# One decoder layer in fp32 products on one core: mixer-norm modulation in quarters, 28 projection units between its loads, and one fp32 product behind each down projection

## The reference

```
mod = silu(c) @ w_mod + b_mod                 # c: 2048, w_mod: 2048 x 12288
sh_a, sc_a, g_a, sh_f, sc_f, g_f = split(mod, 6)
hmix = rms_norm(x, gain) * (1 + sc_a) + sh_a  # 512 x 2048
proj = hmix @ w_in                            # split into u, gla_q, gla_k, gla_v, gla_g, gla_low,
                                              # nsa_q, kc, vc, ksl, vsl, kwn, vwn, nsa_g
mix  = concat(pool_mixer(u), gated_linear_attention(...), nsa_attention(...)) @ w_out
x = x + g_a * mix
hf = rms_norm(x, gain_f) * (1 + sc_f) + sh_f
x = x + g_f * ((silu(hf @ w_gate) * (hf @ w_up)) @ w_down)      # hidden width 5632
```

## Time and profile before

| | us |
|---|---|
| median of 3 runs (2625.59 to 2627.77) | 2626.35 |
| the profiled execution | 2625.79 |
| its span, first to last instruction | 2623.9 |
| TensorE busy | 2488.2 |
| VectorE, ScalarE, GpSimd busy | 893.6, 779.3, 1148.0 |

### The profile page before, as it was taken

One profiled execution on the slowest core, in us unless ns is written; L12 is line 12 of the kernel. 1 busy time (PEld: TensorE's weight loads), 2 busy tenths in 40 slices (PEclk: granted clock), 3 DMA queues, 4 the chain that ended last, 5 costly groups with the idle time before them and its releaser, 6 DMA issues.

```text
span 2623.9 us, 33211 instructions
## 1 busy us (share of the span) xinstructions
PE 2488.2 (95%) x11481; PEld 2028.5 (77%) x11481; DVE 893.6 (34%) x1413; ACT 779.3 (30%) x1482; POOL 1148.0 (44%) x894
## 2 busy tenths in 40 slices
PE   5589999999789999979999999999999999999999
PEld 3577777887688888858888888888888888888887
DVE  4765332258576677771202020201020202010102
ACT  2023224232456622233222222222222222222221
POOL 0024323444576634434444444444444444444443
PEclk8579999999799999989999999999999999999999
DMA  8742223365211177742232323322332332332333
GB/s 298 258 147 81 64 68 103 113 237 180 85 49 57 65 250 256 259 159 95 97 97 96 95 89 96 96 89 94 96 90 94 96 94 90 96 96 89 95 96 112
DMA packets 86221, 315.96 MB, mean 120 GB/s; under 512 B 9584, under 2 KB 10240, under 8 KB 84736
## 3 DMA queue, kind: packets, MB, share of 16 engines
q1 hardware_dynamic: 84240, 303.31, 35.5%
q10 hardware_dynamic: 1904, 11.62, 1.2%
HBM read 310.69 MB, written 4.19 MB: 120 GB/s over the span
## 4 chain that ended last, share of the span: by engine, by line
PE 63%; issue 24%; POOL 10%; DVE 2%; ACT 0%; POOLq 0%; ACTq 0%; DVEq 0%
PE ps L429 57%; POOL wlo L342 9%; PE ps L769 2%; PE ps L758 1%; PE ps L726 1%; PE ps L727 1%; DVE macc L1203 1%; POOL qn L362 0%; DVE biasT L1490 0%; PE ps L712 0%; PE ps L750 0%; POOL kn L367 0%; POOLq L341 0%; PE ps L741 0%; POOL pmod L385 0%
## 5 line engine op out<-in xcount | busy, mean ns | idle before, releaser
L342 POOL TENSOR_TENSOR wlo<-raw,whi 128x512 fp32r<-128x512 f32 x728 | 964.0, 1326 | 1365.5 <-ACT whi L894 1103.2
L894 ACT ACTIVATE whi<-raw 128x512 fp32r<-128x512 f32 x612 | 385.9, 632 | 1260.6 <-PE ps L429 1127.7
L429 PE MATMUL ps<-hfH,whi 128*128 128x512 f32 x1408 | 559.0, 397 | 17.1 <-DVE hfL L1620 13.1
L429 PE MATMUL ps<-hfL,whi 128*128 128x512 f32 x1408 | 558.8, 397 | 0.0
L429 PE MATMUL ps<-hfH,wlo 128*128 128x512 f32 x1408 | 558.3, 397 | 0.0
L429 PEld LDWEIGHTS ps<-hfH,whi 128*128 128x128 f32 x1408 | 266.5, 189 | 80.8 <-issue 13.9
L429 PEld LDWEIGHTS ps<-hfH,wlo 128*128 128x128 f32 x1408 | 266.4, 189 | 61.4
L429 PEld LDWEIGHTS ps<-hfL,whi 128*128 128x128 f32 x1408 | 266.6, 189 | 60.9
L1647 DVE SCALAR_TENSOR_TENSOR x1T<-ps,modc,x1T 128x512 f32<-128x512 f32 x176 | 132.1, 751 | 455.9 <-PE ps L429 455.9
L429 PE MATMUL ps<-huH,whi 128*128 128x512 f32 x704 | 279.2, 397 | 0.5 <-DVE huL L1631 0.5
L429 PE MATMUL ps<-huL,whi 128*128 128x512 f32 x704 | 279.1, 396 | 0.0
(11 more groups left out here) (262 smaller groups left out, 2926.7 us busy)
## 6 DMA issues: line engine op xcount, KB each, us to landing
raw<-in_wstream SPq DMA_DIRECT2D x370, 512.0 KB, 3.6
modw<-in_mstream SPq DMA_DIRECT2D x192, 512.0 KB, 4.6
xT<-in_xt SPq DMA_DIRECT2D x4, 1024.0 KB, 8.2
w1s<-in_w ACTq DMA_DIRECT2D x2, 2048.0 KB, 8.3
x1T<-in_xt ACTq DMA_DIRECT2D x4, 1024.0 KB, 8.6
out_y<-x1T SPq DMA_DIRECT2D x16, 256.0 KB, 2.0
cmpb<-in_cmp_tab ACTq DMA_DIRECT2D x1, 1024.0 KB, 7.1
ptab<-in_tabs ACTq DMA_DIRECT2D x1, 768.0 KB, 5.1
```

The lines of the kernel that those rows point to most:

```text
L342: nc.gpsimd.tensor_tensor(wlo[:, s, :], raw[:, r, :], whi[:, s, :].bitcast(F32), ALU.subtract).then_inc(unit_ready, 1)
L429: ins = nc.tensor.matmul(acc, lhs, rhs, start=first and n == 0, stop=last and n == 2)
L894: A(whi[:, k % SPLIT, :], raw[:, k % 8, :], ACT.Copy).then_inc(unit_hi, 1)
```

## The change

- **Order of the modulation.** The quarters now come as shift 0, scale 0, shift 1, scale 1 and so on, so that after two quarters (16 tiles) four row blocks of x can be modulated.
- **Who computes.** Of each of the 64 tiles VectorE takes only one half of 512 columns (`pre_mod`). Of the other half TensorE takes 128 columns with one product. For the other 384 ScalarE multiplies in place (`scale_rows`) and GpSimd adds into `pacc2` (`add_scaled`). A quarter is closed by seven products in place of four. The accumulators are double.
- **The ring.** It has eight tiles (`modw` and `modx`); a place comes free when VectorE, TensorE and GpSimd are done with it. `scale_rows` stands on ScalarE behind the root L905.
- **Units between loads.** 28 units stand ahead of the blocks: per four row blocks 4 units of gla_q and gla_k, one narrow unit and 2 units of kc. Twenty of them stand between the tiles, from tile 20 on, seven to sixteen tiles (`STEP_UNIT`), their splits on ScalarE and GpSimd two tiles later (`STEP_SPLIT`). 13 unit loads stand between the tile loads on SyncE's queue (`UNIT_LOADS`). The other eight units follow. The fourth block shrinks to 8 units for vc alone, with two `beside` calls behind each.
- **`keep_busy`.** Behind each tile without a unit TensorE makes fp32 products of ones by ones, 128 x 64 by 128 columns, into an unused part of PSUM: six each for tiles 8 to 15, then three each.
- **FFN.** Behind the down projection of each of the ten rounds TensorE makes one fp32 product of identity and ones into bank 1, ahead of the up tile. It waits for `up_saved` at the value for which the up tile waits anyway.
- The five loads of tables on ScalarE's queue move from behind L905 to behind the last rounding of x.

```diff
+        STEP_UNIT = {16 * (u // 7 + 1) + (4, 6, 8, 11, 13, 15, 17)[u % 7]: u for u in range(20)}
+        STEP_SPLIT = {step + 2: u + 4 for step, u in STEP_UNIT.items() if step + 2 < 64}
+        STEP_SPLIT.update({10 + u: u for u in range(4)})
+        UNIT_LOADS = (8, 10, 14, 18, 22, 26, 35, 40, 44, 49, 53, 57, 60)
...
+            def load_pre(m):
+                if m >= 8:
+                    sp.wait_ge(mod_used, m - 7)
+                    sp.wait_ge(mod_pe, m - 7)
+                    sp.wait_ge(mod_pool, m - 7)
+                sp.dma_start(pre_tile(m), mstream[m * P:(m + 1) * P, :]).then_inc(pre_landed[m % 8], 16)
...
+            def add_scaled(m):
+                q, d = m // 8, m % 8
+                if d == 0 and q >= 2:
+                    pool.wait_ge(mod_summed, q - 1)
+                pool.wait_ge(mod_scaled, m + 1)
+                src = pre_tile(m)[:, P:U]
...
+                    ins = TT(pacc2[q % 2][:, :], pacc2[q % 2][:, :], src, ALU.add)
+                ins.then_inc(mod_pool, 1)
+            for m in range(64):
+                add_scaled(m)
+                if m in STEP_SPLIT:
+                    low_part(STEP_SPLIT[m])
...
+            def keep_busy(count):
+                for n in range(count):
+                    nc.tensor.matmul(ps[64:128, 4, 0:P], ones[:, 0:64], ones[:, :], start=True, stop=True,
+                                     skip_group_check=True)
...  in modulate(q), on TensorE:
+                    nc.tensor.matmul(acc[:, 0:1], pre_tile(m)[:, 0:P], cact[:, 2 * d:2 * d + 1], start=d == 0, stop=False,
+                                     skip_group_check=True).then_inc(mod_pe, 1)
                     if beside is not None:
                         beside(d)
+                    elif m in STEP_UNIT:
+                        first_unit(STEP_UNIT[m])
+                    else:
+                        keep_busy(6 if m < 16 else 3)
                 pe.wait_ge(mod_used, 8 * q + 8)
...  four products with pacc, then
+                pe.wait_ge(mod_pool, 8 * q + 8)
+                for j in range(3):
+                    ins = nc.tensor.matmul(acc[:, 1 + j:2 + j], pacc2[q % 2][:, j * P:(j + 1) * P], ones[:, 0:1],
+                                           start=False, stop=True, skip_group_check=True)
...
                 gate_tile(base, 4 * j + 4, 0)
                 down_tiles(base + 4, j)
+                pe.wait_ge(up_saved, 4 * j + 3)
+                nc.tensor.matmul(ps[:, 1, 0:P], ident[:, :], ones[:, :], start=True, stop=True)
                 up_tile(base + 20, 4 * j + 4, 0)
...  on ScalarE, behind the root L905:
+            def scale_rows(m):
+                act.wait_ge(pre_landed[m % 8], 16 * (m // 8 + 1))
+                part = pre_tile(m)[:, P:U]
+                A(part, part, ACT.Copy, scale=cact[:, 2 * (m % 8):2 * (m % 8) + 1]).then_inc(mod_scaled, 1)
+            for m in range(64):
+                scale_rows(m)
+                if m >= 16 and 2 <= m % 16 < 6:
+                    hm_high(4 * (m // 16 - 1) + m % 16 - 2)
+                if m in STEP_SPLIT:
+                    split(0, STEP_SPLIT[m], STEP_SPLIT[m] + 1)
...  on VectorE:
+            pre_mod(0)
             dve.wait_ge(sq_summed, KD)
             own(V.tensor_scalar(xvar[:, :], ps[:, 0, :], 1.0 / D, EPS, ALU.mult, ALU.add))
             V.reciprocal(xvar[:, :], xvar[:, :]).then_inc(var_ready, 1)
+            pre_mod(1, lambda: pre_columns(0))
+            normalise_rows(0)
+            for kq in range(1, 4):
+                def last_rows():
+                    pre_columns(2 * kq - 1)
+                    modulate_rows(kq - 1)
+                pre_mod(2 * kq, last_rows)
+                normalise_rows(kq)
+                pre_mod(2 * kq + 1, lambda: pre_columns(2 * kq))
+            pre_columns(7)
+            modulate_rows(3)
```

More of the change, by code:

```diff
@@ L30 @@
 FAR = 1e30
-UNITS_IN = 16 + 4 + 8 * KD
+UNITS_IN = 28 + 7 * KD + 8
 UNITS_OUT = 4 * KD
@@ L135, in layer_kernel @@
         modw = at("modw", [P, 4, 2 * U], F32, qk_base)
+        modx = at("modx", [P, 4, 2 * U], F32, xs_base)
         macc = at("macc", [P, U], F32, lg_base)
+        pacc = [at(f"pacc{i}", [P, U], F32, pbase + (40 + 2 * i) * KB) for i in range(2)]
+        pacc2 = [at(f"pacc2{i}", [P, 3 * P], F32, pbase + 44 * KB + i * 1536) for i in range(2)]
         place[0] = pbase + 24 * KB
@@ L449, in token_block, with value_block @@
                     after(k)
[L451 to L456, removed]
+            def value_block(u0, after):
+                for j in range(8):
+                    s = j % SPLIT
+                    pe.wait_ge(unit_ready, u0 + (j + 1))
+                    for kk in range(2):
+                        k = 2 * j + kk
+                        for c in range(2):
+                            if k == 0:
+                                pe.wait_ge(proj_saved, 12 + c + 1)
+                            col = slice((2 * kk + c) * P, (2 * kk + c + 1) * P)
+                            ins = passes(ps[:, c, :], hmH[:, k, :], hmL[:, k, :], whi[:, s, col], wlo[:, s, col],
+                                         False, k == 0, k == KD - 1)
+                            if k == KD - 1 and c == 0:
+                                ins.then_inc(tile_done, 1)
+                    ins.then_inc(unit_used, 1)
+                    after(2 * j)
+                    after(2 * j + 1)
@@ L474, in modulate @@
                 for d in range(8):
[L475 to L479, removed]
+                    m = 8 * q + d
+                    pe.wait_ge(pre_landed[m % 8], 16 * (m // 8 + 1))
@@ L500, in _ @@
             modulate(0, square_pair)
-            with pe.Fori(1, 8) as i:
-                modulate(i)
+            modulate(1)
+            for q in range(2, 8):
+                modulate(q)
+            for u in range(20, 28):
+                first_unit(u)
             def sum_columns(q, bank):
@@ L911, in _ @@
                 act.dma_start(dst, src).then_inc(gla_const, 16)
[L912 to L920 removed]
+            split(0, 23, 29)
             for c in range(4):
@@ new lines, in pre_mod, with pre_columns, modulate_rows @@
+                    dve.wait_ge(mod_used, m + 1)
+                    if d == 1 and inside is not None:
+                        inside()
+            def pre_columns(q):
+                dve.wait_ge(mod_summed, q + 1)
+                V.tensor_tensor(modc[:, 4 * q:4 * q + 4], ps[:, 7, 4 * (q % 2):4 * (q % 2) + 4],
+                                vec[:, V_B + 4 * q:V_B + 4 * q + 4], ALU.add).then_inc(mod_read, 1)
+                dve.wait_ge(mod_read, q + 2)
+            def modulate_rows(kq):
+                own(V.scalar_tensor_tensor(out=acol[:, 4 * kq:4 * kq + 4], in0=modc[:, 8 * kq + 4:8 * kq + 8], scalar=1.0,
+                                           in1=vec[:, V_GMIX + 4 * kq:V_GMIX + 4 * kq + 4], op0=ALU.add, op1=ALU.mult))
+                dve.wait_ge(xn_ready, 4 * kq + 4)
+                for k in range(4 * kq, 4 * kq + 6):
+                    if k < 4 * kq + 4:
+                        V.tensor_scalar(xT[:, k, :], xT[:, k, :], acol[:, k:k + 1], modc[:, 8 * kq + k % 4:8 * kq + k % 4 + 1],
+                                        ALU.mult, ALU.add).then_inc(hm_full, 1)
+                    if k >= 4 * kq + 2:
+                        dve.wait_ge(hm_hi, k - 1)
+                        V.tensor_tensor(hmL[:, k - 2, :], xT[:, k - 2, :], hmH[:, k - 2, :].bitcast(F32),
+                                        ALU.subtract).then_inc(hm_ready, 1)
@@ L1234, in _, with normalise_rows @@
+            def normalise_rows(kq):
+                dve.wait_ge(std_ready, 1)
+                for k in range(4 * kq, 4 * kq + 4):
+                    V.tensor_tensor(xT[:, k, :], xT[:, k, :], xrstd[:, :], ALU.mult).then_inc(xn_ready, 1)
             dve.wait_ge(cact_ready, 1)
-            with dve.Fori(0, 2) as i:
-                own.enter(i, 8)
-                half_mod(i)
-            own.leave(2)
+            pre_mod(0)
             dve.wait_ge(sq_summed, KD)
```

261 lines of the change are left out of this document (147 added, 114 removed).

## The result

| | before | after |
|---|---|---|
| median (4 runs each, same chip) | 2627.06 us | 2599.93 us |
| lowest to highest | 2625.59 to 2630.04 | 2594.21 to 2602.03 |
| profiled execution, its span, mean granted clock | 2625.8, 2623.9, 0.962 | 2594.2, 2592.4, 0.977 |

The ratio is 0.9892, 95% interval [0.9876, 0.9907]: 27.1 us faster. The forecast gain was 54.4 us, with a range of 2558 to 2597, which the median misses by 3 us.

A forecast was written before the change was run, and what follows sets the result against it. TensorE was taken as the bound, its large work held back until 156.56 us by the ring of four tiles. 2625.8 - 44 (modulation) - 13.4 (FFN pace) + 3.0 (products) = 2571.4, stated as 2572 us; range 2558 to 2597.

The forecast's parts named there:

- Until tile 8: Start of the kernel: tile 8 can't load before about 41.8 us; GpSimd's eight steps end at 49, quarter 0 at 50.4.
- Tiles 8 to 19: Modulation ahead of the units: quarter 1 closed at 66.9 us, about 4 us more, unit 0 starting at 71 us.
- Tiles 20 to 63: Tiles with units between: 87.3 us of TensorE at full clock plus 6 us of waits, ending at 164.3 us.
- lumps of 1.5 and 0.5 us: TensorE's waits in tiles 20 to 63: 1.5 us for each of three quarters, 0.5 for the other three, 6 us.
- Behind them: From the tiles' end at 164.3 us: unit 20 in effect at 168.3 against 212.93, a gain of about 44 us.
- the three terms of the forecast: Behind the tiles: unit 21 waiting for rows 1 us, five loads delaying unit 23's split 2 us, kc copies 1 us.
- The FFN: Ten FFN rounds: faster pace in eight stretches gains 13.4 us, the fp32 products cost 3.0 us.
- Rival 1: FFN: the product does not reset the pace and 3.0 us are paid for nothing; 2585 us, chance 0.21.
- Rival 2: Modulation: VectorE and GpSimd become the bound, about 22 us of the gain go; 2594 us, chance 0.12.
- a third of a lock: VectorE's multiply-adds beside GpSimd: 1.11 us against 0.75, read as a partial exclusion and not a whole one.
- Rival 3: TensorE's clock stays at half from tile 8 to the tiles' end, 102 us more; 2674 us, chance 0.04.
- Rival 4: TensorE waits less than counted, GpSimd at 0.75 us and no waits at quarter ends; 2560 us, chance 0.07.

The follow-up runs named there:

- experiment 5: Changed kernel with ScalarE scaling the first eight tiles between its squares instead of behind the root: 2592.33 us.
- Experiment 4: Changed kernel with VectorE reading the even quarter's columns before it normalises the rows: 2591.68 us.
- experiment 3: Changed kernel without the 120 idle products of ones by ones: 2585.78 us.
- experiment 7: Changed kernel without idle products, with columns read before the normalisation and the first eight tiles scaled between the squares: 2572.59 us.
- experiment 8: Changed kernel with columns read before the normalisation and the first eight tiles scaled between the squares, idle products kept: 2587.32 us.
- experiment 1: Kernel before with only the ten fp32 products of identity and ones behind the down projections added: 2615.92 us.
- experiment 2: Kernel before with only the wait for up_saved, 2631.7 us; and with ten fp32r products in place of fp32 ones, 2608.1 us; single runs.
- experiment 6: Changed kernel with GpSimd's 56 additions cut from 384 to 8 columns, leaving out the rest of its sums: 2589.84 us.
- the fp32r kernel: Kernel before with ten fp32r products of hfH behind the down projections: 2608.1 us in its single run.

## Why the prediction was half right

**Until tile 8: right.** Forecast: tile 8 at 41.8, GpSimd's sum at 49. Measured 40.78 and 48.70. That `scale_rows(0)` stands behind the root and blocks SyncE was shown by experiment 5. Also right was that the ring frees the loads: 388 GB/s.

**Tiles 8 to 19: 6.3 us short.** Unit 0 came at 77.27, not 71. Closing quarter 1 began at 67.23, where I had 65.5, and took 2.05 us and not 1.4. Steps 16 to 19 took 69.28 to 77.27 = 8.0 us instead of 4, since the clock was at its half level from 69.8 to 80.1 us. I had it at full from about 54 us to the end.

**Tiles 20 to 63: the step that failed.** Forecast 93.3 us (87.3 of work at full clock and 6 of waits), measured from unit 0 to unit 20 194.72 - 77.27 = 117.5. The missing 24.1 us, by distances from start to start:

| part | forecast | measured | more |
|---|---|---|---|
| clock at half for 23.3 of the 117.5 us | 0 | five units of 3.7 to 4.6 us in place of 2.83, and steps beside them | 8.2 |
| waits of TensorE | 6 | 8.3 for columns (5 times) + 4.8 for pacc (twice) = 13.1 | 7.1 |
| tile products and idle products, at full clock | 8.8 + 15.1 | 29.6 | 5.7 |
| units, at full clock | 55.0 | 20 of 2.83 = 56.6 | 1.6 |
| closing a quarter (six times), without its waits | 8.4 | 9.9 | 1.5 |

The waits were a term that I gave in lumps of 1.5 and 0.5 us and never traced. The first product of quarter q + 1 waits at L564 for the columns of the quarter before it to be read; VectorE reads them at step 1 of its own next quarter, and in the odd ones it has four rows to normalise ahead of that. VectorE's timeline in after:

```profile
125.50 3.97 DVE L1377 TENSOR_TENSOR xT<-xT,xrstd 128x512 f32<-128x512 f32 x4
129.40 0.47 DVE L1343 TENSOR_SCALAR pacc<-modw,cact 128x512 f32<-128x512 f32 x1
129.91 0.75 DVE L1345 SCALAR_TENSOR_TENSOR pacc<-modw,cact,pacc 128x512 f32<-128x512 f32 x1
130.69 0.16 DVE L1355 TENSOR_TENSOR modc<-ps,vec 128x4 f32<-128x4 f32 x1
```

The normalisation is 0.99 us a row, not 0.7, and TensorE, which has its sum done at 127.25, goes on at 130.91. Experiment 4 takes that wait away.

The next were the idle products and the clock. I sized the products at 0.21 us and counted 15.1 us of them, which was a price on the bounding engine, and then let the clock stay up for it. In the trace it is 0.80 us at full clock from the first of three to the tile product behind them, 0.27 each, and the clock fell all the same, each time behind the closing of a quarter or a wait there. Three stretches of after:

```profile
107.50:110.90 3.40, 3.40 (x13) 2.70 (x12) 3.40 (x5) 1.66 (x3) 1.71 (x2) 0.52 0.76 237
...
128.00:134.80 6.80, 3.89 (x10) 3.20 (x11) 6.54 (x11) 0.00 (x0) 0.00 (x0) 0.51 0.68 243
...
172.40:179.20 6.80, 4.29 (x11) 3.50 (x12) 6.52 (x11) 0.00 (x0) 0.00 (x0) 0.51 0.53 215
```

Experiments 3, 7 and 8 show that the sum with them is dearer than without, by 8 to 10 us up to the token blocks and by 14 and 15 us in the medians, clock included.

**Behind them: right in size by luck.** Forecast a cost of 4 us; unit 20 stands 18.2 us ahead of the 212.93 of the earlier trace rows, and at w2s 13.4 are left: 4.8. But the three terms of the forecast hardly came. The eight units from 194.72 to 216.88 take 2.77 us each without a wait, so the wait of unit 21 and the five table loads cost nothing; the copies of kc cost 0.85 us, at 220.68. At the fourth block's end TensorE waits 2.9 us for xs, where before waited 2.2, so costing it at nothing was right within the 1 us that I gave. All its waits from there to w2s are 4.1 us against 3.4 before. The rest is the clock, at half from 223.4 to 226.9 and from 441.9 to 448.7 us with 9.5 us of work in it; before had full clock there.

**The FFN: right.** Rounds of 133.12 us from start to start; before, 132.88 and 132.86 and then 134.59. Forecast 13.4 - 3.0 = 10.4, measured 10.4. The price of a round is 133.12 - 132.88 = 0.24 us against the 0.3 taken.

**The rivals.** Rival 1, that the product resets nothing, is refuted by experiments 1 and 2. The Trainium skill, TensorE: Matmul & The Clock Gate, section "Back-to-back issue gap", gives about 0.131 us for 512 columns in a sustained stream and 0.216 us for an isolated matmul; the streams traced here have 0.2289 and 0.2333 and neither of the page's. Rival 2 was the nearest, with 22 us lost for 26 measured at unit 20 and 31 at w2s. Its mechanism is there, but only where GpSimd works: 29 of the 56 multiply-adds of this form ran at 0.74 to 0.77 us, nearly all with GpSimd idle, and 20 at 1.37 to 1.75. Their average of 1.04, near the 1.11 that I used, hides both. Where GpSimd is busy without a gap, four of them take 5.67 us. The first of the four, with GpSimd's instructions beside it, ends 0.55 us behind the end of the one that was under way:

```profile
163.18 1.74 POOL L382 TENSOR_TENSOR wlo<-raw,whi 128x512 fp32r<-128x512 f32 x1
163.80 1.67 DVE L1345 SCALAR_TENSOR_TENSOR pacc<-modx,cact,pacc 128x512 f32<-128x512 f32 x1
164.88 1.46 POOL L396 TENSOR_TENSOR pacc<-pacc,modx 128x384 f32<-128x384 f32 x1
```

GpSimd's instructions stretch too, from 1.29 to 1.74 and from 0.99 to 1.46 us. The rule of the Trainium skill (SBUF — State Buffer, "SBUF: two separate sides") that the two engines shut each other out agrees with these rows, and my reading of 1.11 against 0.75 as "a third of a lock" was wrong: it averaged locked and free instructions. Of the 195 multiply-adds of L1203 in before, from which the 1.11 of the earlier trace rows was taken, 126 last 0.75 us and 65 last 1.5 to 1.9. What did not come is the price that rival 2 put on it. VectorE is busy 72.1 of the 117.6 us, well under TensorE, and by experiment 6 GpSimd's additions are worth at most 6.5 us there. (Its 44 us per 16 tiles were set against 35; the 93.3 us for 44 tiles give 34, so by its own working it would have lost 28 us and not 25.) Rival 3, the clock, happened in small: 0.90 over the 117.6 us and not 0.50, at a price of some 8 us and not 87. Rival 4 is refuted by the waits.

The range failed since its upper end, but for 3 us of room, was rival 2 alone. Waits, the clock and dearer steps each fell on the slow side, and I had treated them as one choice and not as terms that add.

## To carry to other kernels

When a change overlaps stages, write out for every product on the bounding engine which value it waits for and what the engine that makes it does just before; a lump for "waits" hid 7 of 24 us here, and a clock taken as full hid 8. Products that only keep TensorE busy are work on the bounding engine: price them at their measured distance and try the kernel without them. A long stream of equal matmuls that has the slower of two paces can be reset by one short product ahead of it.

## What the runs showed of the hardware

- **Two paces, kept through a stretch.** Matmuls of split operands follow each other at 0.2289 or 0.2333 us at full clock, and a stretch of 384 keeps one. A single 128-column product, fp32 or fp32r, ahead of it gives the faster one every time (87.99 and 87.96 us for 384 with the product's own delay; ten rounds of ten in after, as in experiment 1 and in the fp32r kernel); a wait alone does not. What sets the slower pace after the second round stays open.
- **The clock falls under a busy TensorE.** From 69.8 to 80.1 us it was at 1.2 GHz while the engine's records fill 15.0 of the 15 us from 70 to 85. It had risen with the idle products at 56.2 us and fell behind the seven one-column products that close the quarter and 0.33 us of idle time.
- **VectorE beside GpSimd.** The same 512-column multiply-add takes 0.75 us alone and in most cases 1.37 to 1.75 us beside a GpSimd at work, whose instructions are stretched as well. One VectorE operation of 0.61 us lasted 4.35 us, over five GpSimd instructions; such a delay stands in nine of the 13 traces and not in the other four, with the same code around it.
- **The same code from w2s to hf took 583.5 to 592.5 us** across kernels that differ only elsewhere: 583.5 to 585.2 without that event and 588.2 to 592.5 with it. A gain of some microseconds made ahead of it can shrink or grow there, as in experiment 8.
